# VectorE makes all low parts of the weights; GpSimd keeps the modulation products and sums

## What is computed

```
first block, each of 2 layers
  x += 0.5 * (silu(a) * b) @ w_down        a, b = rmsnorm(x) @ w_up      (width 2816)
  x += mixer(rmsnorm(x))                   q, k, v, glu, gates = h @ w_in + b_in
       three groups of dilated window attention (rms norm of q and k per head, rotation),
       a gated depthwise convolution of 31 taps, layer norm, silu, projection,
       a gated sum of both, and an output projection
  x += 0.5 * (silu(a) * b) @ w_down ;  x = rmsnorm(x)
second block, each of 2 layers
  mod = silu(c) @ mod_w[i] + mod_b[i]      six vectors of 1024: shifts, scales, gates
  h = rms_norm(x) * (1 + sc) + sh ;  y = mixer(h) ;  x += (1 + g) * rms_norm(y)
  h = rms_norm(x) * (1 + sc) + sh ;  y = conv_ffn(h) ;  x += (1 + g) * rms_norm(y)
```

## Time and profile before

| | |
|---|---|
| median of 3 runs | 2698.08 us (2697.8 to 2703.37) |
| span of the profiled execution | 2699.4 us; no other time of this execution is given |
| TensorE / VectorE / ScalarE / GpSimd busy | 90% / 69% / 44% / 38% |
| low parts | 442 on VectorE, 221 on GpSimd |
| modulation products / sums on GpSimd | 96 / 84 |

### The profile page before, as it was taken

One profiled execution on the slowest core, in us unless ns is written; L12 is line 12 of the kernel. 1 busy time (PEld: TensorE's weight loads), 2 busy tenths in 40 slices (PEclk: granted clock), 3 DMA queues, 4 the chain that ended last, 5 costly groups with the idle time before them and its releaser, 6 DMA issues.

```text
span 2699.4 us, 45800 instructions
## 1 busy us (share of the span) xinstructions
PE 2440.6 (90%) x17794; PEld 2347.4 (87%) x17794; DVE 1856.6 (69%) x2446; ACT 1194.6 (44%) x1720; POOL 1029.9 (38%) x501
## 2 busy tenths in 40 slices
PE   7998887998999999887898899898789799897998
PEld 7998777998998999877798899798677799897997
DVE  5667899766666666899975677573734488756555
ACT  5444342254444444443235444435323365543654
POOL 3655443054665566443125466221100122221222
PEclk9999898599999999999679999899655799998999
DMA  6665434045665565533214566343200155443552
GB/s 249 211 221 187 148 126 133 1 164 172 210 228 192 177 227 210 182 135 133 78 59 168 165 224 219 115 158 124 93 9 0 65 178 185 148 149 101 184 182 101
DMA packets 110412, 405.77 MB, mean 150 GB/s; under 512 B 12256, under 2 KB 12384, under 8 KB 109920
## 3 DMA queue, kind: packets, MB, share of 16 engines
q1 hardware_dynamic: 96192, 352.33, 38.5%
q0 software_dynamic: 13824, 50.34, 5.8%
q10 hardware_dynamic: 288, 1.57, 0.2%
HBM read 403.14 MB, written 1.05 MB: 150 GB/s over the span
## 4 chain that ended last, share of the span: by engine, by line
PE 66%; DVE 20%; issue 8%; POOL 3%; ACT 2%; DMA 0%; POOLq 0%; DVEq 0%; SPq 0%; ACTq 0%
PE bank L537 64%; DVE arena L1461 6%; DVE w_lo L1304 4%; PE bank L649 2%; POOL w_lo L467 1%; DVE arena L1506 1%; POOL mod_acc L502 1%; POOL mod_w_buf L494 1%; DVE arena L1511 1%; DVE rinv L1338 1%; DVE work L1342 1%; DVE work L1374 0%; DVE arena L1700 0%; DVE arena L1515 0%; DVE arena L1509 0%
## 5 line engine op out<-in xcount | busy, mean ns | idle before, releaser
L537 PE MATMUL bank<-h_hi,w_hi 128*128 128x256 f32 (+1 forms) x4016 | 1184.4, 295 | 124.2 <-DVE w_lo L1304 64.2
L537 PE MATMUL bank<-h_lo,w_hi 128*128 128x256 f32 (+1 forms) x4016 | 1160.8, 289 | 0.0
L537 PE MATMUL bank<-h_hi,w_lo 128*128 128x256 f32 (+1 forms) x4016 | 1159.4, 289 | 0.0
L467 POOL TENSOR_TENSOR w_lo<-w_raw,w_hi 128x1024 fp32r<-128x1024 f32 x221 | 551.7, 2496 | 1577.5 <-ACT w_hi L982 1576.9
L982 ACT ACTIVATE w_hi<-w_raw 128x1024 fp32r<-128x1024 f32 x663 | 700.1, 1058 | 784.7 <-PE bank L537 782.4
L537 PEld LDWEIGHTS bank<-h_hi,w_hi 128*128 128x128 f32 x4016 | 794.3, 198 | 144.2 <-DVE w_lo L1304 57.4
L1304 DVE TENSOR_TENSOR w_lo<-w_raw,w_hi 128x1024 fp32r<-128x1024 f32 x442 | 688.4, 1564 | 331.7 <-ACT w_hi L982 328.0
L537 PEld LDWEIGHTS bank<-h_lo,w_hi 128*128 128x128 f32 x4016 | 797.3, 199 | 5.7 <-issue 5.5
L537 PEld LDWEIGHTS bank<-h_hi,w_lo 128*128 128x128 f32 x4016 | 795.8, 198 | 0.0
L1461 DVE SCALAR_TENSOR_TENSOR arena<-arena,vecs 128x256 f32<-128x256 f32 x520 | 316.8, 672 | 0.0
L537 PE MATMUL bank<-hid_hi,w_hi 128*128 128x256 f32 x1056 | 297.9, 282 | 3.1 <-DVE hid_lo L1390 3.1
(11 more groups left out here) (205 smaller groups left out, 2093.2 us busy)
## 6 DMA issues: line engine op xcount, KB each, us to landing
w_raw<-weights SPq DMA_DIRECT2D x663, 512.0 KB, 3.4
mod_w_buf<-mod_w POOLq DMA_DIRECT2D x96, 512.0 KB, 4.0
tabs<-shape_tables SPq DMA_DIRECT2D x1, 1746.0 KB, 14.6
work<-v_bias ACTq DMA_DIRECT2D x2, 768.0 KB, 5.1
x<-x_fm SPq DMA_DIRECT2D x1, 1024.0 KB, 4.9
out_fm<-x SPq DMA_DIRECT2D x1, 1024.0 KB, 3.9
vecs<-vectors SPq DMA_DIRECT2D x1, 712.0 KB, 8.3
tabs<-shape_tables SPq DMA_DIRECT2D x1, 65.0 KB, 4.8
```

Source lines behind the costliest of these rows:

```text
L467: nc.gpsimd.tensor_tensor(w_lo[:, SPLIT - 1, :], w_raw[:, n % RAW, :], w_hi[:, SPLIT - 1, :].bitcast(F32), ALU.subtract).then_inc(lo_ready ...
L537: ins = pe.matmul(o, lhs, rhs, start=start, stop=stop, skip_group_check=share)
```

## The change

GpSimd's function `low_part`, its calls between the modulation products and sums, and its loop for the rest of the tiles are taken out. VectorE's `low_parts` makes the low part of each tile, in the place of its program where it passed over every third. The products, sums, loads and waits of the modulation are the same, in the same order, and so are buffers and semaphores.

```diff
@@ gpsimd
-            state = {"tile": SPLIT - 1}
-            def low_part():
-                n = state["tile"]
-                pool.wait_ge(hi_ready, w.next(hi_ready, SPLIT))
-                nc.gpsimd.tensor_tensor(w_lo[:, SPLIT - 1, :], w_raw[:, n % RAW, :],
-                                        w_hi[:, SPLIT - 1, :].bitcast(F32), ALU.subtract
-                                        ).then_inc(lo_ready[SPLIT - 1], 1)
-                state["tile"] += SPLIT
...
                     for kt in range(KT):
-                        low_part()
...
                         pool.wait_ge(pool_link, w.next(pool_link))
-                        if kt % 2 == 0:
-                            low_part()
...
-            done = 24 * DEPTH * MOD_PARTS // 2
-            left = (N_TILES - (SPLIT - 1) + SPLIT - 1) // SPLIT - done
-            with pool.Fori(0, left // 2) as i:
-                w.turn(i, [(hi_ready, 2 * SPLIT)])
-                low_part()
-                low_part()
-            w.turned(left // 2)
-            if left % 2:
-                low_part()
@@ vector, low_parts(upto)
-                    if n % SPLIT == SPLIT - 1:
-                        w.skip(hi_ready, 1)
-                    else:
-                        dve.wait_ge(hi_ready, w.next(hi_ready))
-                        v.tensor_tensor(w_lo[:, n % SPLIT, :], w_raw[:, n % RAW, :],
-                                        w_hi[:, n % SPLIT, :].bitcast(F32), ALU.subtract
-                                        ).then_inc(lo_ready[n % SPLIT], 1)
+                    dve.wait_ge(hi_ready, w.next(hi_ready))
+                    v.tensor_tensor(w_lo[:, n % SPLIT, :], w_raw[:, n % RAW, :],
+                                    w_hi[:, n % SPLIT, :].bitcast(F32), ALU.subtract
+                                    ).then_inc(lo_ready[n % SPLIT], 1)
                     state["split"] += 1
```

More of the change, by code:

```diff
@@ L512, in _ @@
             with pool.Fori(1, DEPTH * MOD_PARTS // 2) as i:
-                w.turn(i - 1, [(hi_ready, 24 * SPLIT), (mod_col_full, 2), (mod_w_full[0], 128), (mod_w_full[1], 128),
+                w.turn(i - 1, [(mod_col_full, 2), (mod_w_full[0], 128), (mod_w_full[1], 128),
                                (pool_link, 28), (mod_acc_ready, 2)])
```

## The result

The changed kernel takes 2822.46 us (median of 4, 2819.67 to 2823.95) against 2699.39 us before (median of 4 runs): a ratio of 1.0452, 95% interval 1.0437 to 1.0467. That is 123 us slower where 50 were forecast.

A forecast was written before the change was run, and what follows sets the result against it. TensorE was taken to bound the feed-forward and VectorE S1 and S2, with short norm chains where TensorE waits. Terms 20 + 17 + 8 + 4 + 1 = +50 us on 2698 gave 2748 us, range 2692 to 2800.

The forecast's parts named there:

- S1 and S2: First half of each layer's first mixer block (229 to 460, 1082 to 1312 us), bound by VectorE: +10 us each, +20.
- The bounds of 1.2 and 2.0 us an operation: Limits on how long each product or sum blocks VectorE in S1 and S2, taken as 1.7 us.
- Norm chains: Norms right behind readings at 665, 866 to 879 and 1519 us: products and sums block their instructions, +17 us, bounds 0 and 30.
- Feed-forward under a burst: Feed-forward stages beside bursts: TensorE hides most VectorE delays, +4 us over some 240 us of bursts, bounds 0 and 25.
- The sign that I had named: The prediction is wrong if feed-forward stages beside a burst lose over 5% of TensorE.
- the sum of needs: In the feed-forward, VectorE's 4.9 us and GpSimd's 5 to 6 us of the same lock exceed 8.8 us for three tiles.
- The start: Before the reading at about 225 us: no term of its own; the first two parts run from about 25 to 115 us.
- Mixer tails: Parts beginning at 595 and 1445 us run beside splits that TensorE waits for: +4 us each, +8, bounds 0 and 16.
- The rest: After 1740 us GpSimd has no products; one or two low parts enter the recurrence's VectorE chain: +1 us, bounds -3 and +4.
- the first: Rival: VectorE becomes the bound in the feed-forward too, 36 to 60 us more, about 2800 us; chance 0.14.
- The second, the freed lock: Rival, in S1 and S2: the lock is freed, bursts do no harm, norms take nothing; 2678 us, chance 0.13.
- The exchange of low parts: In S1 and S2, 18 low parts cost VectorE about 27 us by blocking, 20 to make: gains 7 us a stretch.

The follow-up runs named there:

- e4_after_norm_gate: The changed kernel, but each modulation part from the third on waits for the high part of the fourth tile after the reading that lets it start; 2788.79 us.
- the paced kernel: The kernel before with all 663 low parts on VectorE, GpSimd's products and sums still waiting for every third high part; 2680.73 us, ratio 0.993.
- 2607 against 2623: The changed kernel and the kernel before, each with modulation products and sums over 16 columns instead of 1024; 2607.01 and 2622.9 us.
- quarters: The changed kernel with each modulation product and sum in four instructions of 256 columns; 2742.82 us.
- e6_one_burst: All low parts on VectorE, all modulation parts gated at the pace of the kernel before, except the seventh, which runs freely; 2702.04 us, ratio 1.0009.

## Why the prediction was wrong

The direction and the mechanism were right: GpSimd's products lose their pace, run in bursts behind the readings, and VectorE stands behind them where it is waited for. The size was not: 2748 forecast, 2822 measured, over the range's 2800. Term by term:

- *S1 and S2, +20.* Measured -12.0 + 16.3 - 9.9 + 15.0 = +9.4, the norms ahead of both included. The form was as forecast, free in the middle and worse at both ends. The bounds of 1.2 and 2.0 us an operation give -3 and +21 for a stretch, not the -11 and +29 stated; the measured +4.3 and +5.1 lie inside either.
- *Norm chains, +17.* This is the step that failed. The sentence "a product, a product and a sum (1.9 + 1.9 + 2.45) fall into 6 us of chain" counted what fits into the chain's old length. But the chain grows while it stands, and more operations fall into it: of the burst, four k-tiles go by. I had the number beside it, a lock held about 70% of the time, and did not carry it through: 16 instructions with two to four let through in each 5.7 us make over 20 us. The norm groups stand 80 us more over five chains, 16 each, where I had 5. For the three chains of this term and the final norm that is 3 x 16 + 5.1 = 53 us of VectorE's time against 17.
- *Feed-forward under a burst, +4.* Failed too. The stages of norm and feed-forward together lose 21.8 + 5.1 + 35.0 + 18.3 = 80 us; three chains of 16 make 48 of it at most, so some 30 lie in the final norm and the feed-forward. Seen from TensorE, its waits for the norms' `h_lo` in the three stages go from 7.6 to 48.4 us and those for low parts from 2.1 to 17.6, and it is busy 17 us longer for the same work, at a granted clock of 0.95, 0.91 and 0.95 against 0.98, 0.99 and 0.98. No term had a price for the clock; beside the norm chain from 937 to 965 us TensorE is busy 11.4 of 28 us at a granted clock of 0.50, its lower level of 1.2 GHz. With the norms clean, `e4_after_norm_gate` shows the share of the feed-forward: the three stages take 211.9, 221.9 and 211.6 us where the paced kernel takes 200.3, 200.9 and 203.1, 41 us in all, part of which may come from the shorter rests of a written-out program. The sign that I had named, over 5% of TensorE lost beside a burst, came true: 4 of 50 us. That TensorE bore 3.6 us of one late `hid_lo` was no evidence for many in a row; the sum of needs, which I had as over the 8.8 us, was the better sign.
- *The start, counted within those 4.* +17.4. I did not look at what VectorE runs there: a chain of small instructions that took 2.4 us before and 13.1 beside the burst (27.47 to 40.60 us).
- *Mixer tails, +8.* Measured 10.7 + 7.6 = +18.
- *The rest, +1.* Measured -3.6.

The sum of the measured terms is 9.4 + 80.2 + 17.4 + 18.3 - 3.6 = 121.7 us.

Of the rivals, the first (VectorE bound in the feed-forward under a burst, about 2800) came nearest: both it and the forecast's mechanism happened, each at a part of its price. The second, the freed lock, is real but belongs to another kernel: forecast 2678, and the paced kernel takes 2681. Its condition, norm chains that stay as they are, is just what the pace gives. That the two numbers lie so close is luck in part: by the readings the stretches gain 10 and 6 us of it and the start, which that rival did not have, 5.5. The exchange of low parts, 20 us a stretch for 27 of blocking, was confirmed by 2607 against 2623: between these two kernels the stretches differ by 6.5 and 4.4 us, where 7 each were forecast.

The Trainium skill, page "SBUF — State Buffer", section "SBUF: two separate sides", says that whichever of the two starts first gets the shared pair for the whole instruction and the other blocks fully. That the other blocks fully agrees with the 2.57 us of a norm instruction of 0.47 at 704.87. That the first to start gets the pair does not agree with every row: the instruction of 708.10 started 0.32 us ahead of the product and stood for the whole of it, and with quarters the one of 678.09 stood through four GpSimd instructions, 2.94 us, though it had started ahead of all of them.

## What to carry to other kernels

Two engines that exclude each other need a pace, not only a balance: the waits that an operation had by accident of its place in the program were worth 142 us here, and taking out the work between them took out the pace. When a stretch of dependent small instructions meets a burst, don't count the operations that fit into its old length; divide its instructions by those let through in one period of the burst (here 16 by 4, at 5.68 us a period). A wait on a counter of the main stream (here the high parts) is a cheap way to place side work, and cutting that work into shorter instructions limits what one collision costs.

## What the runs showed of the hardware that was not expected

- Total standing and lost time can go opposite ways: three main groups of VectorE stood 368 us before and 160 after (240 with the norms), and the kernel became 123 us slower.
- A norm instruction of VectorE that starts during GpSimd's issue of a load (0.59 us), with a product right behind the issue, stands through the whole product: 2.52 us for one of 0.41. Where no product follows at once, instructions run within the issue in 0.47 and 0.41 us (`e6_one_burst`).
- In the norm chains one waiting VectorE instruction passes between a product of GpSimd and its sum, which are linked by a semaphore and 0.08 us apart. Between quarters without one, sometimes one passes at each (0.94 us), sometimes none in four (2.94 us). What decides it stays open.
- The rest of GpSimd between a sum and the issue of a load is 0.65 us in a loop with a register address and 0.30 us in a program written out. A norm chain of 16 instructions beside the burst takes 21.9 us with the first and 28.2 with the second.
